# A hybrid encoder block on one core: the two attention stages as one program over blocks of three query chunks

## The reference

```python
scale_g = 1.0 / float(np.sqrt(GQA_HEAD_DIM))          # 64
def attend_gqa(qb):
    qb = qb.reshape(B, Q_BLOCK, GQA_KV_HEADS, rep, GQA_HEAD_DIM)      # 2 key heads, rep = 4 query heads each
    s = jnp.einsum('bqgrd,bkgd->bgrqk', qb, k_g, preferred_element_type=jnp.float32) * scale_g
    p = jax.nn.softmax(s, axis=-1).astype(v_g.dtype)
    o = jnp.einsum('bgrqk,bkgd->bqgrd', p, v_g)
...
scale_m = 1.0 / float(np.sqrt(MLA_NOPE_DIM + MLA_ROPE_DIM))           # 96
def attend_mla(qb):                                                   # 8 heads, each with keys of its own
    s = (jnp.einsum('bqhd,bkhd->bhqk', qn, k_nope, preferred_element_type=jnp.float32)
         + jnp.einsum('bqhd,bkd->bhqk', qr, k_rope, preferred_element_type=jnp.float32)) * scale_m
    p = jax.nn.softmax(s, axis=-1).astype(v_m.dtype)
    o = jnp.einsum('bhqk,bkhd->bqhd', p, v_m)
```

## Time and profile before

| | |
|---|---|
| median of 3 runs | 3435.21 us (3434.39 to 3437.47) |
| profiled execution, first to last instruction (span) | 3443.7 us |
| mean granted TensorE clock over the span | 0.929 |
| busy, share of the span | PE 89%, PEld 82%, DVE 59%, ACT 45%, POOL 15% |
| attention, first score matmul to last finishing step | 563.86 to 1751.70 us |

### The profile page before, as it was taken

How to read it: one execution, slowest core, us unless ns; L and a number is a source line. 1 busy time by engine, 2 the same in 40 slices (tenths; PEclk the granted TensorE clock), 3 DMA queues, 4 the chain that set the end, 5 groups by cost and what they waited for, 6 DMA issues and landing times. The chain is left out here.

```text
span 3443.7 us, 64532 instructions
## 1 busy us (share of the span) xinstructions
PE 3070.8 (89%) x21802; PEld 2811.4 (82%) x21802; DVE 2020.9 (59%) x4136; ACT 1549.7 (45%) x3358; POOL 533.6 (15%) x715
## 2 busy tenths in 40 slices
PE   5999586999997999999969999997991799999990
PEld 4888575888886888888859999996880799999990
DVE  4788455888885767666733333333338455555545
ACT  3333234777775666666622222222111344544532
POOL 0000000222221112212200000000003133333320
PEclk8999798999998999999979999998995899999995
DMA  5555695212213132222266747446652688888847
GB/s 171 168 170 156 177 288 160 94 63 92 93 62 91 35 86 70 62 62 62 67 191 180 222 121 219 122 122 197 193 173 78 169 200 205 200 201 200 206 102 214
DMA packets 597790, 494.44 MB, mean 144 GB/s; under 512 B 51536, under 2 KB 530816, under 8 KB 597680
## 3 DMA queue, kind: packets, MB, share of 16 engines
q1 hardware_dynamic: 583088, 450.55, 46.3%
q0 software_dynamic: 12288, 34.10, 5.6%
q10 hardware_dynamic: 2304, 8.39, 0.6%
HBM read 339.32 MB, written 153.62 MB: 143 GB/s over the span
## 5 line engine op out<-in xcount | busy, mean ns | idle before, releaser
L1443 PE MATMUL c_acc<-c_tokens,c_w_hi 128*128 128x260 f32 x2048 | 375.9, 285 | 30.1 <-DMA c_tokens<-hn_t 29.3
L1443 PEld LDWEIGHTS c_acc<-c_tokens,c_w_hi 128*128 128x128 f32 x2048 | 319.0, 190 | 30.8 <-issue 21.8
L1507 DVE TENSOR_TENSOR c_w_lo<-c_raw,c_w_hi 128x1536 fp32r<-128x1536 f32 x64 | 112.5, 1759 | 311.6 <-ACT c_w_hi L1463 311.6
L1971 PE MATMUL e_gu<-e_x_hi,w_hi 128*128 128x260 f32 x1024 | 293.7, 287 | 0.9 <-DVE e_x_lo L2114 0.9
L1443 PE MATMUL c_acc<-c_tokens,c_w_lo 128*128 128x260 f32 x1024 | 290.9, 284 | 0.0
L1971 PE MATMUL e_gu<-e_x_lo,w_hi 128*128 128x260 f32 x1024 | 289.6, 283 | 0.0
L1971 PE MATMUL e_gu<-e_x_hi,w_lo 128*128 128x260 f32 x1024 | 289.3, 283 | 0.0
L2109 DVE TENSOR_TENSOR w_lo<-w_raw,w_hi 128x2048 fp32r<-128x2048 f32 x90 | 206.3, 2292 | 103.5 <-ACT w_hi L2047 102.8
L1046 PE MATMUL m_s_ps<-m_k,m_q 96*128 96x512 f32 (+1 forms) x864 | 249.5, 427 | 15.4 <-DMA m_k<-mk_t 15.4
L1216 DVE TENSOR_REDUCE m_peak<-m_s_ps 128x1 f32<-128x1024 f32 x144 | 176.1, 1223 | 126.8 <-PE m_s_ps L1046 123.6
L1463 ACT CAST c_w_hi<-c_raw 128x1536 fp32r<-128x1536 f32 x64 | 94.8, 1481 | 288.0 <-DMA c_raw<-in_w_o_gqa 252.5
(11 more groups left out here) (261 smaller groups left out, 8274.7 us busy)
## 6 DMA issues: line engine op xcount, KB each, us to landing
c_raw<-in_w_in SPq DMA_DIRECT2D x64, 512.0 KB, 5.3
w_raw<-in_w_gate SPq DMA_DIRECT2D x64, 512.0 KB, 6.7
w_raw<-in_w_up SPq DMA_DIRECT2D x64, 512.0 KB, 8.4
w_raw<-in_w_down SPq DMA_DIRECT2D x64, 512.0 KB, 4.5
g_k<-gk_t SPq DMA_DIRECT2D x32, 520.0 KB, 5.4
c_tokens<-hn_t SPq DMA_DIRECT2D x16, 1040.0 KB, 9.6
c_tokens<-o_t SPq DMA_DIRECT2D x32, 520.0 KB, 7.8
r_mt<-mix_t SPq DMA_DIRECT2D x32, 512.0 KB, 5.2
```

What stands on the lines that cost most here:

```text
L1443: pe.matmul(acc[:, b, mixer, 0:W], w[:, parity, mixer, k, :], tokens[:, t % 2, part, k, cols], start=(k == 0 and at == 0), stop=(k == DK - ...
L1507: dve.tensor_tensor(w_lo[:, parity, mixer, :, :], raw[:, mixer, :, :], w_hi[:, parity, mixer, :, :].bitcast(F32), ALU.subtract).then_inc(p ...
L1971: ins = pe.matmul(gu[:, j % 2, a, 0:W], w[:, j, at:at + P], t[:, k, :], start=(k == 0 and q == 0), stop=(k == DK - 1 and q == 2))
```

## The change

`attend` is replaced by one stage `attention` (tiles named t_) that does both attentions.

- A unit of the grouped-query part is now one group and one key head with its four query heads: 32 chunks of 128 queries, and one chunk of 64 that holds the 16 extra queries of the four heads, 33 chunks. A unit of the latent part stays one head and one group, nine chunks. There are 4 + 16 units and 276 chunks (288 before).
- Three chunks in a row are a block, 92 in all, 384 columns wide but for the last block of a unit (320 or 272). Queries' and probabilities' tiles are laid out by block; `pt_hi` and `pt_lo` have two buffers of a block each.
- The 16 extra keys are now a key tile of 128 partitions: their high half at partition 0, their low half at partition 32, zeros elsewhere, with the values twice. POOL makes the halves (`split_meta`) ahead of the transposes (`meta_transposes`). So a block has 16 value products and one for the extra keys, 17.
- The products with the extra keys are made for each block (`meta_scores`); POOL adds the bias to them (`shift`), and ACT takes one exponential of them per block (`meta_exp`). Sums and reciprocals are one step per block on DVE (`totals`).
- The scale of the scores is put on the queries: in `project` into the gain of the query heads, in `latents` in the copy of the queries out of PSUM (L807).
- The reciprocal sums' transposes (`scale_rows`) go to a bank of the ring `tp`, not to `o_ps`.
- All engines' programs are written out; there is no loop. SP stores each block when it is finished.

The core of the diff (the old `attend` is above; its removed lines are left out):

```diff
--- before.py
+++ after.py
...
+                        dve.tensor_scalar(head_gain[:, 0:HEADS, :], head_gain[:, 0:HEADS, :], HD ** -0.5, None, ALU.mult)\
+                            .then_inc(gain_scaled, 1)
+                        dve.wait_ge(gain_scaled, 1)
...
-                    dve.tensor_copy(qm[0:r, g, :, :].rearrange("p (a h) d -> p a (h d)", a=2), acc[0:r, 0:2, 0:384])\
-                        .then_inc(up_dve, 1)
+                    dve.tensor_scalar(qm[0:r, g, :, :].rearrange("p (a h) d -> p a (h d)", a=2), acc[0:r, 0:2, 0:384],
+                                      QK_M ** -0.5, None, ALU.mult).then_inc(up_dve, 1)
...
+def attention(nc, io, scr):
+    MIXERS = 2
+    QUADS = HEADS // KV
     CH = XCH + 1
+    PER = 3
     RING = 3
+    WIDE = PER * P
+    G_Q = QUADS * TOK
+    M_AT = 32
+    PAIR = M_AT + META
+    units = [(0, g, kv) for g in range(GROUPS) for kv in range(KV)]
+    units += [(1, g, h) for h in range(HEADS) for g in range(GROUPS)]
+    chunks = []
+    for u, (mla, g, h) in enumerate(units):
+        if mla:
+            chunks += [(u, c * P, META if c == XCH else P) for c in range(CH)]
+        else:
+            chunks += [(u, c * P, QUADS * META if c == QUADS * XCH else P) for c in range(QUADS * XCH + 1)]
+    N = len(chunks)
+    BLOCKS = N // PER
...
+    order = [("meta_scores", 0)]
+    for b in range(BLOCKS):
+        for i in range(PER):
+            n = b * PER + i
+            if i == 1 and b + 1 < BLOCKS:
+                order.append(("meta_scores", b + 1))
+            order += [("x", n, 0), ("x", n, 1)]
+        order.append(("meta", b))
+        if b > 0:
+            order.append(("scales", b - 1))
+    order.append(("scales", BLOCKS - 1))
+    number = {kind: f for f, kind in enumerate(order)}
...
+            load_qk(0)
+            sp.wait_ge(zeros_ready, 4)
+            load_v(0)
+            for b in range(BLOCKS):
+                u = unit_of(b)
+                starts = first_block[u] == b and u + 1 < len(units)
+                if starts:
+                    load_qk(u + 1)
+                if b > 0:
+                    store(b - 1)
+                if starts:
+                    load_v(u + 1)
+            store(BLOCKS - 1)
...
+            def bank_free(f):
+                if f >= RING:
+                    if order[f - RING][0] == "x":
+                        pe.wait_ge(tp_lo, x_until[f - RING + 1])
+                    else:
+                        pe.wait_ge(tp_act, f - RING + 1)
...
+            def values(b, tiles):
+                u, w, p = unit_of(b), width(b), unit_of(b) % 2
+                if tiles[0] == 0:
+                    if b == first_block[u]:
+                        pe.wait_ge(v_loaded[p], v_after[u])
+                    if b > 0:
+                        pe.wait_ge(o_summed, b)
+                    pe.wait_ge(tp_lo, lo_count(b * PER + PER - 1))
+                for kk in tiles:
+                    if kk == XCH:
+                        pe.wait_ge(tp_act, number["meta", b] + 1)
+                        pe.matmul(o_ps[:, 0:w], v[:, p, kk, :], pt_meta[:, b % 2, 0:w], start=False, stop=True)\
+                            .then_inc(o_filled, 1)
+                    else:
+                        pe.matmul(o_ps[:, 0:w], v[:, p, kk, :], pt_hi[:, b % 2, kk, 0:w], start=(kk == 0), stop=False)
+                        pe.matmul(o_ps[:, 0:w], v[:, p, kk, :], pt_lo[:, b % 2, kk, 0:w], start=False, stop=False)
...
+            PARTS = [[0, 1], [2, 3, 4], [5, 6, 7, XCH]]
+            scores(0)
+            meta_scores(0)
+            scores(1)
+            pe.wait_ge(zeros_ready, 4)
+            for n in range(N):
+                b, i = n // PER, n % PER
+                if n + 2 < N:
+                    scores(n + 2)
+                if i == 1 and b + 1 < BLOCKS:
+                    meta_scores(b + 1)
+                transposes(n)
+                if i == PER - 1:
+                    meta_transposes(b)
+                if b > 0:
+                    values(b - 1, PARTS[i])
+                    if i == PER - 1:
+                        scale_rows(b - 1)
+            for part in PARTS:
+                values(BLOCKS - 1, part)
+            scale_rows(BLOCKS - 1)
...
+            def evacuate(b):
+                f, w = number["scales", b], width(b)
+                act.wait_ge(o_filled, b + 1)
+                if b >= 2:
+                    act.wait_ge(scaled, b - 1)
+                act.copy(low_half[:, b % 2, 0:w], o_ps[VD:P, 0:w]).then_inc(o_act, 1)
+                act.wait_ge(tp_filled, f + 1)
+                act.copy(scales[:, b % 2, 0:w], tp[0:VD, f % RING, 0:w]).then_inc(tp_act, 1)
...
+            act.wait_ge(zeros_ready, 4)
+            meta_copy(0)
+            softmax(0)
+            for n in range(N):
+                b, i = n // PER, n % PER
+                if n + 1 < N:
+                    softmax(n + 1)
+                if i == 0 and b >= 2:
+                    evacuate(b - 2)
+                if i == 1:
+                    if b + 1 < BLOCKS:
+                        meta_copy(b + 1)
+                    meta_exp(b)
+                hi(n)
+                if i == PER - 1:
+                    meta_rows(b)
+            evacuate(BLOCKS - 2)
...
+            def totals(b):
+                dve.wait_ge(exp_done, (b + 1) * PER)
+                dve.wait_ge(meta_exp_done, b + 1)
+                if b >= 2:
+                    dve.wait_ge(tp_filled, number["scales", b - 2] + 1)
+                for r, which in edges(b):
+                    ins = dve.tensor_reduce(total[0:r, b % 2, which], mp[0:r, b % 2, which, :], AX_X, ALU.add)
+                ins.then_inc(total_done, 1)
+                dve.wait_ge(total_done, b + 1)
+                for r, which in edges(b):
+                    ins = dve.reciprocal(inverse[0:r, b % 2, which], total[0:r, b % 2, which])
+                ins.then_inc(inverse_done, 1)
+            def sum_halves(b):
+                w = width(b)
+                if b >= 2:
+                    dve.wait_ge(out_done, b - 1)
+                dve.wait_ge(o_act, b + 1)
+                dve.tensor_tensor(summed[:, b % 2, 0:w], o_ps[0:VD, 0:w], low_half[:, b % 2, 0:w], ALU.add)\
                     .then_inc(o_summed, 1)
+            peaks(0)
+            meta_peak(0)
+            biases(0)
+            peaks(1)
+            biases(1)
+            for n in range(N):
+                b, i = n // PER, n % PER
+                if n + 2 < N:
+                    peaks(n + 2)
+                    if i == 1:
+                        meta_peak(b + 1)
+                    biases(n + 2)
+                if i == 0 and b >= 2:
+                    sum_halves(b - 2)
+                lo(n)
+                if i == PER - 1:
+                    totals(b)
+            sum_halves(BLOCKS - 2)
+            sum_halves(BLOCKS - 1)
...
+            def split_meta(b):
+                pool.wait_ge(meta_exp_done, b + 1)
+                if b >= 2:
+                    pool.wait_ge(tp_filled, number["meta", b - 2] + 1)
+                for r, which in edges(b):
+                    ins = pool.tensor_copy(pair[0:r, b % 2, which, 0:META], mp[0:r, b % 2, which, 0:META])
+                ins.then_inc(pair_hi_done, 1)
+                pool.wait_ge(pair_hi_done, b + 1)
+                for r, which in edges(b):
+                    ins = pool.tensor_tensor(pair[0:r, b % 2, which, M_AT:PAIR], mp[0:r, b % 2, which, 0:META],
+                                             pair[0:r, b % 2, which, 0:META].bitcast(F32), ALU.subtract)
+                ins.then_inc(pair_done, 1)
...
+            for b in range(BLOCKS):
+                shift(b)
+                split_meta(b)
+                if b >= 2:
+                    finish_block(b - 2)
+            finish_block(BLOCKS - 2)
+            finish_block(BLOCKS - 1)
...
-        attend(nc, io, scr, False)
-        attend(nc, io, scr, True)
+        attention(nc, io, scr)
```

More of the change, by code:

```diff
@@ L954, in attend, with runs @@
-        LOADS = 16 * (4 if mla else 3)
+        qk_total, v_total, store_total = [0, 0], [0, 0], [0, 0]
+        qk_after, v_after = [], []
+        for u, (mla, _, _) in enumerate(units):
+            qk_total[u % 2] += 16 * 4
+            v_total[u % 2] += 16 * 3
+            qk_after.append(qk_total[u % 2])
+            v_after.append(v_total[u % 2])
+        def runs(b):
+            u = unit_of(b)
+            mla, g, h = units[u]
+            out, at = [], 0
+            for n in range(b * PER, (b + 1) * PER):
+                start, r = chunks[n][1], rows(n)
+                if mla:
+                    pieces = [(h, start, r)]
+                elif r == P:
+                    pieces = [(h * QUADS + start // SEQ, start % SEQ, r)]
+                else:
+                    pieces = [(h * QUADS + j, SEQ, META) for j in range(QUADS)]
+                for head, to, w in pieces:
+                    if out and out[-1][0] == head and out[-1][1] + out[-1][2] == to:
```

(50 more changed lines are left out.)

533 lines of the change are left out of this document (193 added, 340 removed).

## The result

The changed kernel takes 3358.8 us (median of 4 runs, 3358.52 to 3361.49) against 3434.82 of the kernel before: a ratio of 0.978 [0.977, 0.980], 76 us less. 3372 was forecast, within 3320 to 3425.

The account below looks back on a forecast made before the run. TensorE was taken to bound attention: 973 us of work, 137 of waiting for DVE's sum and 15 at the ends make 1125 against 1187.8, 63 less; off the 3435.2 median that is 3372 us, range 3320 to 3425.

Parts of the forecast that it names:

- The wait: Ahead of each block's first value products TensorE stands still for DVE's sum: 1.49 us in each of 92 blocks, 137 us.
- The links: From first transpose to value product: peak 0.20 us, bias 1.26, next DVE step 0.13, sum 0.55, product 0.14; 2.28 in all.
- The work: TensorE's matmuls and transposes in attention's 92 blocks at full-clock prices: 954 us, taken as 973.
- the 2%: TensorE prices summed over the old attention units came out 2% low, so 2% was added: 954 became 973 us.
- The ends: Attention's start and end: longer first loads 6 us, filling 2, half clock at first 5, wider last block 2; 15 in all.
- The clock: Full clock in attention after its first stretch; 64 us back, already in the sum.
- the first rival: The clock falls in every block, next to the stall: 1.7 us each, 156 us in all 92, 3528 us; chance 9%.
- The second rival: The sum's place in DVE's order costs nothing, TensorE has no idle time ahead of value products: 3235 us; chance 8%.
- the third: A wait priced at nothing is late, latent loads behind a store or POOL's split: 46 to 48 us, 3420; chance 11%.
- my 3381: Forecast for the whole profiled execution: its span of 3443.7 us before the change, with 63 us taken off.

Follow-up runs that it names:

- the kernel with the sum first: The changed kernel with sum_halves(b-2) ahead of peaks and biases in DVE's order at each block's first chunk, instead of behind them: 3234.09 us, 0.941 of the kernel before.

## Why the prediction was right

Attention with its load was forecast at 1125 us and took 1100.6 + 4.6 = 1105.2; the 20 us between are in three terms.

- **The wait.** Place and releaser were as said, and the number, 91 for 92. Its size was 1.36 to 1.39 us, not 1.49: 124 instead of 137 us. The links were right to 0.01 us but for one. From the sum's end to PE's product I took 0.14, and it is 0.05. The row was not an odd one, as another such wait of the kernel before (product at 1087.75) shows 0.14 too; the distance goes with the width of the sum. In the profile after it is 0.05 behind sums of 384 columns and 0.10 behind those of 320 and 272. From the start of the sum to the product it is 0.56 with 256 columns and 0.59 with 384: I priced these two links at 0.69. Why the added columns cost so little stays open.
- **The work.** Prices held: value products 0.175, a grouped-query block 11.12 us in the timeline against 11.2. From 1100.6 come off 124 for the wait, 4 for half clock at the start (half of 8.3 us) and 4 for filling and last block, which are the forecast's own and not measured; some 968 are left where I had 973. The bare sum was 954, so 1.5% was missing, not 2. It was not missing everywhere, as the kernel with the sum first shows, where no wait is in the way: a full grouped-query block takes 9.69 (priced 9.71), a latent unit 33.7 (priced 33.04), 11 of the 14 us. So the 2% came out nearly right in the sum and not part by part, which is in part luck.
- **The ends.** 13 instead of 15: the load costs 4.6 instead of 6, the half clock at the start 4 instead of 5.
- **The clock.** Full after the start, as forecast. But the reason that I gave against the first rival (dense products on both sides of the stall) does not hold: with the same products around a longer stall the clock fell. The trace of before could not tell at which length of stall the clock falls, so 9% was a guess. Its price was off as well: 1.7 us for a fall, where the 64 falls behind the longest stall lasted 5.5 us each on average and cost 2.5. As for what the half clock cost before, I wrote 64 us from rounded clocks; stretch by stretch it is 110 us at half clock inside the stages behind the start, 55 lost, and 5 at the start. Nothing hung on it, as the sum was made at full-clock prices.
- **The second rival** (stall hidden, 3235) could not come in this kernel, as DVE's order forbids it; but its time is that of the kernel with the sum first, 3234.1; that the two agree to 1 us is luck, as the terms above and the 8.5 us below were off by more. Of the third there is no sign: the next largest wait in attention is 2.6 us in all.

The median came out 13 under the forecast, where the profile is 21 under my 3381: the profiled execution of before lay 8.5 us over its median, that of after 0.9. So that the median came nearer is luck. (The upper end of the forecast's own range adds up to 3413, not 3410; nothing hung on it.)

So the change is right in what it removes and pays 124 of 211 us (1187.8 - 976.5) back at one line of DVE's order. The extra queries' shared chunk, the width and the clock have runs of their own; what the missing seam and the joined extra keys gave was not measured apart.

## What to carry to other kernels

When the profile shows one engine as the bound, follow each single-buffered hand-over (here o_ps) through the order of the other engine: a short step that frees a buffer belongs ahead of a step that waits for the bound engine's newest result, not behind it. Where that engine has idle time before its wait, as DVE had here, the move costs nothing. And a stall on TensorE can have two prices, its own length and the clock behind it. Look at both: here the second was nothing at 1.39 us, came behind 11 of 91 stalls at 1.99, and behind 64 at 2.59.

## What the runs showed of the hardware

- With the same products around it, an idle TensorE was followed by the lower clock more often the longer it stood: after 0, 11 and 64 of 91 stalls of 1.39, 1.99 and 2.59 us. A stretch at half clock cost 0.45 of its length in both kernels that had them.
- A TensorE that is busy throughout can lose its clock too: behind the 16-column products, 3.40 busy of 3.40 us, it went to 0.50, and with 128 columns, at the same 0.111 us each, the grouped-query stretch stayed at 1.00. Widening these products cost no time and gave clock.
- At the upper clock a value product costs 0.111 us at 16 and at 128 columns, 0.118 at 256, 0.175 at 384: sixteen times the columns for 6% more time, then half as many again for 48%.
